# A two-layer hybrid encoder trunk on one core: the mixer and the seams between its stages are rewritten, with R0 in front of the P transposes, R1 behind the state updates and the GLA norm's sums behind one output unit

## The reference

```
x += 1/2 * SwiGLU_1(RMSNorm(x))        # 1024 -> 2816 -> 1024
h  = RMSNorm(x)
proj = h @ w_in                        # q k v | q_g k_g v_g gate r_g
A: 8-head sliding-window attention (2 chunks of 64), sinks, ALiBi, then RMSNorm over 512
B: gated linear attention, 4 heads, chunks of 64, state carried over chunks,
   RMSNorm per head, times silu(r_g)
x += concat(A, B) @ w_out
x += 1/2 * SwiGLU_2(RMSNorm(x))
```

## Time and profile before

| | |
|---|---|
| median of 3 runs | 1011.42 us (1007.83, 1011.63, 1011.42) |
| profiled execution | 1007.62 us, span of its instructions 1005.7 us |
| PE, DVE, ACT, POOL busy | 972.5, 628.4, 457.2, 55.8 us |
| mean granted TensorE clock | 0.979 of full speed |
| DMA | 169.13 MB, 168 GB/s over the span |

### The profile page before, as it was taken

How to read it: one execution, slowest core, us unless ns; L and a number is a source line. 1 busy time by engine, 2 the same in 40 slices (tenths; PEclk the granted TensorE clock), 3 DMA queues, 4 the chain that set the end, 5 groups by cost and what they waited for, 6 DMA issues and landing times.

```text
span 1005.7 us, 20058 instructions
## 1 busy us (share of the span) xinstructions
PE 972.5 (97%) x8116; PEld 959.1 (95%) x8116; DVE 628.4 (62%) x743; ACT 457.2 (45%) x499; POOL 55.8 (6%) x37
## 2 busy tenths in 40 slices
PE   7999999989999999999979999998999999999996
PEld 6999999989999999999979999998998999999996
DVE  7755555667778655555665555557595785555553
ACT  5443434536645443434534343435475544343432
POOL 4000000030101000000120000003001010000000
PEclk8999999989999999999999999999998999999997
DMA  7665656544335665655446556555442556565621
GB/s 259 219 207 169 206 169 209 169 127 126 85 98 197 211 199 174 193 183 185 149 137 218 197 177 198 177 200 155 140 105 63 170 167 210 168 199 175 190 102 43
DMA packets 130621, 169.13 MB, mean 168 GB/s; under 512 B 3217, under 2 KB 116113, under 8 KB 130577
## 3 DMA queue, kind: packets, MB, share of 16 engines
q1 hardware_dynamic: 130576, 168.52, 53.0%
HBM read 167.46 MB, written 1.05 MB: 168 GB/s over the span
## 4 chain that ended last, share of the span: by engine, by line
PE 77%; issue 14%; DVE 4%; POOL 3%; DMA 1%; ACT 1%; SPq 0%; DVEq 0%; ACTq 0%; POOLq 0%
PE ps L358 25%; PE ps L359 25%; PE ps L360 25%; POOL sq L1346 2%; DVE xlo L982 2%; PE ps L668 1%; DVE wlo L977 1%; PE ps L664 1%; DMA raw<-in_ffn_w_gate 1%; DMA raw<-in_ffn_w_up 1%; ACT xhi L770 0%; PE ps L415 0%; POOL sqsum_a L1346 0%; PE ps L738 0%; PE ps L706 0%
## 5 line engine op out<-in xcount | busy, mean ns | idle before, releaser
L977 DVE TENSOR_TENSOR wlo<-raw,whi 128x2048 fp32r<-128x2048 f32 (+1 forms) x159 | 355.6, 2239 | 249.5 <-ACT whi L756 249.5
L358 PE MATMUL ps<-xhi,whi 128*128 128x256 f32 x1760 | 498.7, 283 | 12.8 <-DVE wlo L977 6.1
L359 PE MATMUL ps<-xlo,whi 128*128 128x256 f32 x1760 | 494.5, 281 | 0.0
L360 PE MATMUL ps<-xhi,wlo 128*128 128x256 f32 x1760 | 493.8, 281 | 0.0
L756 ACT ACTIVATE whi<-raw 128x2048 fp32r<-128x2048 f32 (+1 forms) x159 | 297.2, 1869 | 182.7 <-PE ps L360 168.9
L358 PEld LDWEIGHTS ps<-xhi,whi 128*128 128x128 f32 x1760 | 333.6, 190 | 17.2 <-issue 7.1
L359 PEld LDWEIGHTS ps<-xlo,whi 128*128 128x128 f32 x1760 | 333.0, 189 | 0.1
L360 PEld LDWEIGHTS ps<-xhi,wlo 128*128 128x128 f32 x1760 | 332.9, 189 | 0.0
L359 PE MATMUL ps<-h_parts,whi 128*128 128x256 f32 x704 | 196.1, 279 | 0.0
L360 PE MATMUL ps<-h_parts,wlo 128*128 128x256 f32 x704 | 196.1, 278 | 0.0
L358 PE MATMUL ps<-h_parts,whi 128*128 128x256 f32 x704 | 196.0, 278 | 0.0
(11 more groups left out here) (138 smaller groups left out, 525.7 us busy)
## 6 DMA issues: line engine op xcount, KB each, us to landing
raw<-in_ffn_w_down SPq DMA_DIRECT2D x44, 1024.0 KB, 4.9
raw<-in_ffn_w_up SPq DMA_DIRECT2D x43, 1024.0 KB, 5.4
raw<-in_ffn_w_gate SPq DMA_DIRECT2D x42, 1024.0 KB, 5.4
raw<-in_w_in SPq DMA_DIRECT2D x12, 1024.0 KB, 5.2
raw<-in_w_in SPq DMA_DIRECT2D x8, 512.0 KB, 4.5
raw<-in_w_out SPq DMA_DIRECT2D x8, 512.0 KB, 4.3
raw<-in_w_in SPq DMA_DIRECT2D x2, 1088.0 KB, 5.2
raw<-in_ffn_w_gate SPq DMA_DIRECT2D x8, 256.0 KB, 7.0
```

The lines of the kernel that those rows point to most:

```text
L358: pe.matmul(o, w_hi, x_hi, start=start, stop=False, skip_group_check=True)
L359: pe.matmul(o, w_hi, x_lo, start=False, stop=False, skip_group_check=True)
L360: return pe.matmul(o, w_lo, x_hi, start=False, stop=stop, skip_group_check=True)
L977: nc.vector.tensor_tensor(lo, r, h.bitcast(F32), ALU.subtract).then_inc(lo_done, 1)
```

## The change

Eight things change together. (1) The squares: ACT makes two pieces of 128x1024 (`squares`) behind the split of the third unit instead of four of 128x512 inside `gains`; DVE adds them (1024, 512 and 256 wide) behind the split of the second unit; POOL keeps only the first and the last norm. The attention norm's two adds go to DVE too. (2) `square_sums` at the mixer's start moves into the middle of `M_V1`, and the spread of r from the middle of `M_Q0` to its front. (3) `diagonals` goes: `spread` now multiplies a column of r, broadcast over 128 columns, by the float32 identity, one 128-column float32 matmul for each column of r (2, or 8 for the GLA norm) instead of two fp32r matmuls per 256 or 512 columns. (4) Rank-gate transposes move into `M_Q0`; the transposes of v and the gate logits go ahead of `M_Q1` instead of behind it; scores 0 to 2, 3 to 5 and 6 to 7 follow `M_Q1`, `M_QG` and `M_KG` (before: `M_QG`, `M_KG` and `M_V0`); ACT's and DVE's weight splits stand later in their order. (5) The A blocks run as one batch, alternating between the halves of the rows, right behind `M_V0`; the transposes of `kend` behind them; `M_R0` follows, and only then all eight P transposes. (6) ACT copies the first four P, then `ket` and v, then the last four; `M_R1` follows the state updates. (7) The GLA output runs all L664 products first, then the attention spread, then the L668 products, alternating between halves. (8) The attention half of the mixed input is written to the feed-forward's spare buffer; the GLA norm's sums stand behind the first `w_out` unit as before, but write `ps[3]`, and its spread stands behind the second unit instead of inside the third.

```diff
-            def spread(o, n, a, b):
-
-                for part in range(2):
-                    d = diag[:, part * n + a:part * n + b, :].rearrange("p a b -> p (a b)")
-                    last = pe.matmul(o, ones_r[:, :], d, start=part == 0, stop=part == 1, skip_group_check=True)
+            def spread(o, call, y, n):
+
+                pe.wait_ge(rs_step, RS * (call + 1))
+                for i in range(n):
+                    last = pe.matmul(o[i // 4][:, i % 4 * P:(i % 4 + 1) * P], y[:, i:i + 1].to_broadcast([P, P]), ident,
+                                     start=True, stop=True, skip_group_check=True)
                 return last
 
-            def spread_r(v):
-
-                pe.wait_ge(diag_done, v + 1)
...
+            def spread_r(call, y):
+
+                spread([ps[3][:, 256:512]], call, y, TT).then_inc(rb_ps, 1)
...
-                square_sums(v)
-                project_tokens(M_V1, t, [ps[1][:, 0:WIDE], ps[2][:, 0:WIDE]])
+                project_tokens(M_V1, t, [ps[1][:, 0:WIDE], ps[2][:, 0:WIDE]], lambda: square_sums(v))
...
-                project(M_Q0, t, tiles(7), lambda: spread_r(v))
-
-                pe.wait_ge(rb_done, v + 1)
-                pe.wait_ge(lr_tok_ev, 2 * ev)
-                for tt in range(TT):
-                    last = pe.transpose(ps[3][0:RANK, tt * P:(tt + 1) * P], lr_tok[:, tt, :], ident)
-                last.then_inc(lr_ps, 1)
+                spread_r(5 * l + 1, rcol)
...
+                def rank_tokens():
+
+                    pe.wait_ge(rb_done, v + 1)
+                    pe.wait_ge(lr_tok_ev, 2 * ev)
+                    for tt in range(TT):
+                        last = pe.transpose(ps[3][0:RANK, tt * P:(tt + 1) * P], lr_tok[:, tt, :], ident)
+                    last.then_inc(lr_ps, 1)
+
+                project(M_Q0, t, tiles(7), rank_tokens)
...
-                project(M_Q1, t, tiles(0))
...
-                project(M_QG, t, tiles(1))
+                project(M_Q1, t, tiles(0))
...
-                project(M_KG, t, tiles(2))
+                pe.wait_ge(v_ev, 4 * l + 2)
+                project(M_QG, t, tiles(1))
                 pe.wait_ge(q_ev, 2 * l + 2)
                 for s in range(3, 6):
...
-                project_tokens(M_V0, t, [ps[0][:, 0:UC], ps[0][:, UC:2 * UC]])
+                project(M_KG, t, tiles(2))
                 for s in range(6, HEADS):
                     scores(s, l)
+                project_tokens(M_V0, t, [ps[0][:, 0:UC], ps[0][:, UC:2 * UC]])
+
+                pe.wait_ge(va_ev, ev)
...
+                pe.wait_ge(ke_done, ev)
+                pe.wait_ge(qe_done, ev)
+                for j in range(2):
+                    for tt in range(TT):
+                        for h in (2 * j, 2 * j + 1):
+                            b, c = DK * (h % 2), (2 * j + tt) * P
+                            last = pe.matmul(ps[3 + h % 2][:, c:c + P], ke[b:b + DK, j, tt * P:(tt + 1) * P],
+                                             qe[b:b + DK, j, tt * P:(tt + 1) * P],
+                                             start=True, stop=True, skip_group_check=True)
+                            if j == 1 and tt == TT - 1:
+                                last.then_inc(A_ps, 1)
...
-                project(M_R0, t, tiles(1))
...
                 last.then_inc(ket_ps, 1)
-                for s in range(3):
+                pe.wait_ge(kg_ev, ev)
+                project(M_R0, t, tiles(2))
+                for s in range(HEADS):
                     turn_probs(s, l)
...
-                pe.wait_ge(ke_done, ev)
-                pe.wait_ge(qe_done, ev)
-                for h in range(GH):
...
-                    for tt in range(TT):
-                        c = (2 * j + tt) * P
-                        last = pe.matmul(ps[3 + h % 2][:, c:c + P], ke[b:b + DK, j, tt * P:(tt + 1) * P],
-                                         qe[b:b + DK, j, tt * P:(tt + 1) * P],
-                                         start=True, stop=True, skip_group_check=True)
-                    if h >= 2:
-                        last.then_inc(A_ps, 1)
-                    if h:
-                        turn_probs(2 + h, l)
-                for s in range(6, HEADS):
...
                 pe.wait_ge(rg_ev, 2 * l + 1)
-                pe.wait_ge(kg_ev, ev)
+                for h in range(GH):
+                    j = h // 2
+                    for tt in range(TT):
+                        pe.matmul(o_tile(h)[:, tt * P:(tt + 1) * P], vg[:, tt, h * P:(h + 1) * P],
+                                  AT[:, 4 * (h % 2) + 2 * j + tt, :],
+                                  start=(h < 2 and tt == 0), stop=False, skip_group_check=True)
+                spread([ps[3][:, 256:512]], 5 * l + 2, rs_y, TT).then_inc(rA_ps, 1)
+
                 pe.wait_ge(st_done, 5 * ev)
-                for h in range(GH):
...
-                    o = tiles(1 + h % 2)[:, h // 2, :]
-                    for tt in range(TT):
-                        pe.matmul(o[:, tt * P:(tt + 1) * P], vg[:, tt, h * P:(h + 1) * P], AT[:, 4 * (h % 2) + 2 * j + tt, :],
...
-                                last = pe.matmul(o[:, c * CHUNK:(c + 1) * CHUNK], Sta[b:b + DK, c - 1, j, :],
...
-                    if h == 0:
-
-                        pe.wait_ge(adiag_done, ev)
-                        spread(ps[3][:, 256:512], TT, 0, TT).then_inc(rA_ps, 1)
+                for j in range(2):
+                    for c in range(1, NCH):
+                        for h in (2 * j, 2 * j + 1):
+                            b = DK * (h % 2)
+                            last = pe.matmul(o_tile(h)[:, c * CHUNK:(c + 1) * CHUNK], Sta[b:b + DK, c - 1, j, :],
+                                             qe[b:b + DK, j, c * CHUNK:(c + 1) * CHUNK],
+                                             start=False, stop=True, skip_group_check=True)
+                            if j == 1 and c == NCH - 1:
+                                last.then_inc(o_ps, 1)
...
+                def gla_sums():
+
+                    pe.wait_ge(am_done, 4 * l + 2)
+                    pe.wait_ge(osq_done, 2 * ev)
+                    for h in range(GH):
+                        for tt in range(TT):
+                            last = pe.matmul(ps[3][:, 2 * h + tt:2 * h + tt + 1],
+                                             sq[:, 4 + h, tt * P:(tt + 1) * P], ones[:, 0:1],
+                                             start=True, stop=True, skip_group_check=True)
+                    last.then_inc(oss_done, 1)
...
-                        if k == 2:
-
-                            pe.wait_ge(o_ev, 2 * ev)
-                            pe.wait_ge(odiag_done, ev)
-                            for b in range(2):
-                                r = spread(ps[1 + b][:, :], 8, 4 * b, 4 * b + 4)
-                            r.then_inc(rG_ps, 1)
...
-                                                 start=True, stop=True, skip_group_check=True)
-                        last.then_inc(oss_done, 1)
+                        gla_sums()
+                    if i == M_WO + 1:
+
+                        pe.wait_ge(o_ev, 2 * ev)
...
                                              scale=gain[:, m:m + 1]).then_inc(xhi_done, 1)
-                    nc.scalar.activation(sq[:, 2 * p:2 * p + 2, :], resid[:, 2 * p:2 * p + 2, :],
-                                         ACT.Square).then_inc(sq_done, 1)
+
+            def squares():
+
+                for half in range(2):
+                    four = slice(4 * half, 4 * half + 4)
+                    nc.scalar.activation(sq[:, four, :], resid[:, four, :], ACT.Square).then_inc(sq_done, 1)
 
...
 
                 split_mix(2)
+                squares()
...
                 exps(0)
+                split_mix(8)
+                exps(1)
+                for s in range(4):
+                    probs_out(s)
+                act.wait_ge(ket_ps, ev)
+                nc.scalar.copy(ket[:, :, :].rearrange("p a b -> p (a b)"), ps[1][:, :]).then_inc(ket_ev, 1)
                 v_out(M_V0, [ps[0][:, 0:UC], ps[0][:, UC:2 * UC]])
+                for s in range(4, HEADS):
+                    probs_out(s)
                 split_mix(9)
-                exps(1)
-                act.wait_ge(ket_ps, ev)
...
+
                 split_mix(10)
...
-
                 for b in range(2):
                     act.wait_ge(am_done, 4 * l + b + 1)
-                    mixed_hi(b, at32[:, 2 * b:2 * b + 2, :])
...
+
+            def flat(a, b):
+                return sq[:, a:b, :].rearrange("p m t -> p (m t)")
+
+            def sum_squares(v, steps):
+
+                dve.wait_ge(sq_done, 2 * v)
+                nc.vector.tensor_tensor(flat(0, 4), flat(0, 4), flat(4, 8), ALU.add).then_inc(sum_step, 1)
+                dve.wait_ge(sum_step, steps + 1)
+                nc.vector.tensor_tensor(flat(0, 2), flat(0, 2), flat(2, 4), ALU.add).then_inc(sum_step, 1)
+                dve.wait_ge(sum_step, steps + 2)
```

(30 more changed lines are left out.)

191 lines of the change are left out of this document (69 added, 122 removed).

## The result

| | before | after |
|---|---|---|
| median of 4 runs each | 1009.62 us (1005.07 to 1011.63) | 981.57 us (980.44 to 982.21) |
| profiled execution, its span | 1007.62, 1005.7 us | 982.21, 980.4 us |

The account below looks back on a forecast made before the run. PE was taken to bound the kernel, busy 972.5 of 1005.7 us. Terms summed to 16.65 us gained, 991.0 against 1007.6; with 1.5 added for the median the forecast was 992.5, range 988 to 997.

Parts of the forecast that it names:

- What PE waits for: Whole kernel: POOL's last add for the norm is PE's largest releaser, 10.1 us in three waits; POOL busy near 13 after.
- Feed-forward to mixer: Seam from M_KV to M_Q0, twice: no wait in M_V1, 0.95 us before the spread; gain 6.2 each, 12.4.
- Mixer up to `M_R0`, P transposes to updates: Mixer, twice: up to M_R0 nothing; P transposes to updates 10.05 us with a 1.25 us stand, loss 0.4 each, -0.8.
- GLA output: GLA output up to w_out, twice: 6.05 us with PE standing near 2 us; gain 1.2 each, 2.4.
- `w_out` and mixer to feed-forward: Twice each: w_out's dearer GLA spread and a 0.4 us wait, -2.3; faster xlo at mixer to feed-forward, 4.3.
- The seam to the next layer: Feed-forward to the next layer: 13.64 us for work needing 11.9, 0.3 of wait left; gain 1.45.
- rival 2: Jump back at L722 absorbs its seam: 994, or 989 if it shortens too; chance 0.66 together with the forecast.
- Rival 1: Mixer's tail: the lower clock moves there, two spells in each layer, costing 10 us: 1001; chance 0.13.
- Rivals 3 to 5: Sums stay late, 1001, 0.13; 1.2 GHz from P transposes through GLA output, 1025, 0.03; rivals 1 and 3 together, 0.05.
- The runs' median: Whole kernel: median put 1.5 us above the sum, since two of three runs lie 3.8 above the profiled one.

Follow-up runs that it names:

- Experiment 4: New kernel with ACT's copies of ket and v and the split of the first w_out unit ahead of the eight P copies; 977.58 us, ratio 0.9765.
- experiment 6: New kernel with the attention norm's spread ahead of the 16 chunk products of the GLA output instead of behind them; 974.81 us, ratio 0.9703.
- experiment 7: New kernel with DVE's split of the second w_out unit behind the two low parts of the attention half; 975.09 us, ratio 0.9697.
- experiment 9: New kernel with the GLA output's products in the earlier kernel's order, head by head, spread behind the first head; 983.24 us, ratio 0.9809.
- experiment 3: New kernel with one 1 MB weight load issued about 3 us later, in flight at the jump back; 983.18 us, ratio 0.9814.
- experiment 1: New kernel with the seams' sums back on POOL and four 128x512 squares on ACT, all else new; 993.99 us, ratio 0.9923.
- experiment 2: Kernel before with only the sums moved: two squares on ACT, three adds on DVE; 992.53 us, ratio 0.9895.
- experiment 11: The new kernel unchanged, run once more; 979.52 us, ratio 0.9746.
- experiment 10: New kernel with the moves of experiments 4, 6 and 7, plus DVE's two attention norm adds ahead of its gate product; 971.17 us, ratio 0.9668.
- experiment 5: New kernel with M_R0 behind the eight P transposes instead of in front of them; 978.76 us, ratio 0.9722.
- experiment 8: New kernel with the three moves of experiments 4, 6 and 7 together; 973.77 us, ratio 0.9686.
- experiment 12: Experiment 10's kernel with DVE's split of the first w_out unit moved behind its split of M_R1; 969.35 us, ratio 0.9668.

## Why the prediction was right in kind and short in size

*What PE waits for.* Right: the three late sums were the largest cost, and they are gone; POOL is busy 11.3 us (13 forecast).

*Feed-forward to mixer.* Forecast 6.2 each, measured 6.8 and 7.1. DVE, of which the forecast had each step, was 0.5 us quicker relative to `M_V1` than forecast: its root starts 4.5 us behind the start of `M_V1` instead of 5.0, and PE waits 0.4 us in front of the spread instead of 0.95.

The adds took their forecast time, 2.4 us in all. The spread's four records take 0.47 us (0.43 forecast).

*Mixer up to `M_R0`, P transposes to updates.* Cost nothing as forecast; and 8.45 us for P transposes to updates with 1.5 for A and `kend` make 9.95 where 10.05 was forecast. The stand came for the reason given (ACT's copies between P 3 and P 4) and at its size. Experiment 4 confirms the cause.

*GLA output.* 5.87 us where 6.05 was forecast, with the stand of 2 us in it; experiments 6, 7 and 9 confirm both halves, the chain through DVE and the order of shapes.

*`w_out` and mixer to feed-forward.* 2.2 measured, 2.0 forecast. Both terms hold. The spread takes 2.19 us with 0.46 of wait in it, 1.25 more than before (1.15 forecast). Four `xlo` took 4.67 us beside POOL and take 1.66 now:

```profile
303.55 1.66 DVE L986 SCALAR_TENSOR_TENSOR xlo<-resid,par,xhi 128x256 fp32r<-128x256 f32 x4
```

*The seam to the next layer.* This is the step that failed. It was priced as 1.45, 1.25 with its spread: the late sum's wait alone, with the jump's stop and the clock behind it unchanged in the sum. The shorter stop stood only in rival 2, at 989. Measured are 5.7. They divide into three. The late sum gave 2.0 (72 products in 8.48 us instead of 10.36, and 0.1 in the sums). The jump's stop fell from 4.08 to 1.62: 2.5. The lower clock behind it did not follow the shorter stop: the 24 products there took 4.45 us, 16 of them at 0.213 each, and take 2.93, which gives 1.5. The dearer spread and a slightly slower pace take 0.3 off. The weight loads around the branch, before (it starts at 510.18) and after (497.67):

```profile
504.85 0.38 SPq L259 DMA_DIRECT2D raw<-in_ffn_w_down  x1
...
507.10 0.37 SPq L259 DMA_DIRECT2D raw<-in_ffn_w_gate  x1
```

```profile
492.88 0.38 SPq L258 DMA_DIRECT2D raw<-in_ffn_w_down  x1
498.45 0.37 SPq L258 DMA_DIRECT2D raw<-in_ffn_w_gate  x1
```

A load is released by DVE's split of the unit before in its slot. Before, DVE ended two splits back to back beside POOL, and two loads of 1 MB were in flight over the start of the branch. After, the first split comes sooner, the adds for the norm stand between the two, and the loads are 5.6 us apart: the first landed as the branch began (DMA share 0.98 up to 497.6, 0.05 in the 0.8 us behind), the second was issued just behind. That the traffic sets the branch's length is shown by experiment 3. That part (1) of the change is what parts the loads is shown by experiments 1 and 2: with POOL's sums they come back together, with the sums on DVE alone they are apart. By the Trainium skill ("Runtime: NRT & Kernel Launch", Instruction fetch mechanics) a taken branch to a page not held waits for its fetch by DMA. The packet inside each branch agrees. The prediction drew from it that the stop stays whatever DVE does, and that does not follow: in experiment 3 the packet comes 1.7 us later beside a weight load than after, and DVE times the weight loads.

*Rival 1.* The lower clock did not multiply in the profiled execution: one spell, in layer 2's `w_out`, cost 1.8 us, where the one of before cost 3.0. In experiment 11 it came in both layers. The prediction put it down to the new stops; that is shown only in part. In the grouped order it goes away when the stand ahead of `w_out` shrinks, but it also came without any stand there: in both layers of experiment 9, and in one of two of before and of experiment 2 (last section). 10 us it does not cost. Rivals 3 to 5 did not come.

*The runs' median.* 1.5 us were added for runs slower than the profiled one; the new kernel's median lies 0.6 under its profiled run. These 2.1 us and the 8.8 by which the sum was short are the miss of 10.9. Half of the 8.8 is the seam to the next layer (4.4).

*What stays open.* Why the lower clock follows one of two equal stretches. And what length of stop brings it: of two waits in experiment 2 the one of 2.50 us did not and the one of 2.57 did, while at the jump 2.37 us brought it (experiment 2) and 2.18 did not (experiments 7 and 10).

## What to carry to other kernels

A wait that one late engine causes has a price in three places: the wait, the lower clock behind it, and the loads that its neighbours then release late; price all three, and don't add the gains of two remedies for one wait. When a queue of work changes speed, ask which transfers shift with it and what else is on the DMA engines at that moment, instruction fetches among them. Where an engine is idle ahead of a stand that it then causes (ACT for 6.7 us in front of its copies of P, DVE for 7.6 us ahead of the state updates in experiment 10), change the order. Five changes of order together took 7.8 us off what the rewriting had left; the fourth paid only when the fifth had cleared its way.

## What the runs showed of the hardware that was not expected

The jump back of the loop over layers took PE 3.3 to 4.0 us in the eleven profiles in which the DMA engines moved next to nothing in its first microsecond (5 to 27 GB/s), and 4.8 to 5.7 in the three in which a weight load was in flight there (337 to 397 GB/s: before, experiments 1 and 3). Some 1.6 to 1.7 us of it don't show on PE, which still works off what it had been given (5.67 and 4.08 before, 3.33 and 1.62 after).

The lower clock at the end of the GLA output or in `w_out`: in the six profiles where the grouped GLA output ends in the stand of 2.27 us it came in 8 of 12 mixers (after, experiments 1, 3, 4, 5 and 11), at 1.6 to 2.9 us each. In the five with that stand at 1.14 us or less it came in none of 10 (experiments 6, 7, 8, 10 and 12). So with the grouped order, shortening the stand seems to gain more than its length. But a stand is not needed: in the three profiles whose GLA output takes its products in turns and ends in none (before, experiments 2 and 9) it came in 4 of 6 mixers. No run tells what brings it there. This is a count of profiles, not a mechanism.

A feed-forward body takes either 161.7 us or 2.2 to 2.3 more, with the same program and a granted clock of 1.00 in both; the products of `h` with the down weights go at 0.113 us in one and at 0.118 in the other. It was so in 15 of 56 bodies, before and after in 2 of 4 each. No run tells why. One or two slow bodies are 2.2 to 4.5 us, which could be much of what two runs of one kernel differ by; only the profiled runs show it.
